# Two of four weight sums of a pair on GpSimd, with signs turned, and other orders in the pairs and ahead of them

## What is computed

```python
h = rms_norm(x, ffn_norm[layer])
gate, up = jnp.split(h @ w_gate_up[layer], 2, axis=-1)
x = x + (jax.nn.silu(gate) * up) @ w_down[layer]
```

## Time and profile before

| | |
|---|---|
| median of 3 runs | 2815.51 us (2812.23 to 2816.04) |
| the profiled execution | 2812.47 us |
| its span (first to last instruction) | 2810.6 us |
| mean granted TensorE clock | 0.988 |
| busy: PE, DVE, ACT, POOL | 2669.9, 1705.8, 1335.0, 1444.9 us |
| three instructions of a pair's four-sum set on raw weights and `w_sum` (L2131, L2134, L2136) | 114.2, 135.9, 115.9 us |

### The profile page before, as it was taken

How to read it: one execution, slowest core, us unless ns; L and a number is a source line. 1 busy time by engine, 2 the same in 40 slices (tenths; PEclk the granted TensorE clock), 3 DMA queues, 4 the chain that set the end, 5 groups by cost and what they waited for, 6 DMA issues and landing times.

```text
span 2810.6 us, 47222 instructions
## 1 busy us (share of the span) xinstructions
PE 2669.9 (95%) x16306; PEld 2328.5 (83%) x16306; DVE 1705.8 (61%) x2881; ACT 1335.0 (47%) x2426; POOL 1444.9 (51%) x953
## 2 busy tenths in 40 slices
PE   9999899999999899999999998999999999899997
PEld 7877889898878889888878887898987888788886
DVE  6674949477454948465545238584757643776674
ACT  7664535356564535353254335353547443453443
POOL 3654456564454556565446434565654473365653
PEclk9999999999999999999999999999999999999998
DMA  4301222333202222232213321322322341132322
GB/s 177 113 2 53 71 95 91 104 113 108 98 24 71 75 95 101 89 128 86 100 43 129 104 66 48 105 90 97 114 96 91 105 150 46 53 109 77 115 75 90
DMA packets 69276, 252.78 MB, mean 90 GB/s; under 512 B 7680, under 2 KB 7936, under 8 KB 68864
## 3 DMA queue, kind: packets, MB, share of 16 engines
q1 hardware_dynamic: 68112, 247.43, 25.6%
q10 hardware_dynamic: 1008, 3.28, 0.4%
HBM read 248.58 MB, written 2.10 MB: 89 GB/s over the span
## 4 chain that ended last, share of the span: by engine, by line
PE 72%; DVE 14%; issue 8%; ACT 4%; DVEq 0%; DMA 0%; POOL 0%; ACTq 0%; SPq 0%; POOLq 0%
PE ps L747 14%; PE ps L749 14%; PE ps L748 14%; PE ps L1140 6%; PE ps L1144 6%; PE ps L1142 6%; PE ps L914 3%; DVE w_sum L2131 2%; PE ps L952 2%; PE ps L937 2%; DVE ps L2139 1%; ACT ev L1557 1%; PE ps L856 1%; DVE w_sum L2134 1%; PE ps L858 1%
## 5 line engine op out<-in xcount | busy, mean ns | idle before, releaser
L628 POOL TENSOR_TENSOR w_lo<-w_raw,w_hi 128x1024 fp32r<-128x1024 f32 x300 | 725.5, 2423 | 710.9 <-ACT w_hi L1377 682.6
L1377 ACT ACTIVATE w_hi<-w_raw 128x1024 fp32r<-128x1024 f32 x302 | 316.9, 1055 | 313.0 <-PE ps L749 237.7
L674 POOL TENSOR_TENSOR w_lo<-w_raw,w_hi 128x512 fp32r<-128x512 f32 x240 | 348.1, 1465 | 169.4 <-ACT w_hi L1361 169.4
L747 PE MATMUL ps<-xh,w_hi 128*128 128x512 f32 x980 | 389.0, 397 | 11.5 <-POOL w_lo L628 4.8
L1140 PE MATMUL ps<-t_hi,w_hi 128*128 128x256 f32 x1280 | 367.3, 287 | 22.3 <-issue 22.3
L749 PE MATMUL ps<-xh,w_lo 128*128 128x512 f32 x980 | 383.3, 391 | 0.0
L748 PE MATMUL ps<-xl,w_hi 128*128 128x512 f32 x980 | 383.1, 391 | 0.0
L1142 PE MATMUL ps<-t_lo,w_hi 128*128 128x256 f32 x1280 | 366.5, 286 | 0.0
L1144 PE MATMUL ps<-t_hi,w_lo 128*128 128x256 f32 x1280 | 366.1, 286 | 0.0
L674 POOL TENSOR_TENSOR w_lo<-w_sum,w_hi 128x512 fp32r<-128x512 f32 x160 | 208.0, 1319 | 299.9 <-ACT w_hi L1361 299.9
L1140 PE MATMUL ps<-xh,w_hi 128*128 128x256 f32 x960 | 278.6, 290 | 59.8 <-ACT ev L1557 55.0
(11 more groups left out here) (342 smaller groups left out, 5708.3 us busy)
## 6 DMA issues: line engine op xcount, KB each, us to landing
w_raw<-weights_in SPq DMA_DIRECT2D x462, 512.0 KB, 3.3
x<-x_in SPq DMA_DIRECT2D x4, 512.0 KB, 7.9
...
rope<-rope_in SPq DMA_DIRECT2D x1, 512.0 KB, 10.9
...
```

The costliest lines, as they stand in the source:

```text
L628: nc.gpsimd.tensor_tensor(w_lo[:, slot], w_raw[:, slot], w_hi.bitcast(f32)[:, slot], ALU.subtract).then_inc(lo_ready, 1)
L674: last = nc.gpsimd.tensor_tensor(quad(w_lo, name, q), src, quad(w_hi, name, q).bitcast(f32), ALU.subtract)
L747: nc.tensor.matmul(dst, w_hi[:, slot, w], hi, start=first, stop=False)
L1377: A(w_hi[:, s], w_raw[:, s], ACT.Copy).then_inc(hi_ready, 1)
```

## The change

- **The sums.** `quad_lows` on POOL begins each pair with sums 3 and 4 (`sums`, semaphore `raw_sums`); DVE keeps sums 2 and 5 (semaphore `bank_sums`). Sum 3 is now +(a + b) instead of -(a + b), so that a plain TENSOR_TENSOR does; sum 2 comes out as before, sum 5 with its sign turned. Products 3 and 5 so have the other sign, and DVE's additions of `ev[2]` and of bank c become subtractions. The sums of a part's first pair stand on POOL right ahead of its low parts, behind the low parts of the chunks before.
- **ACT in a pair.** `ev[2]` is copied right after `ev[1]`; then come `ahead(2)`, `ahead(3)` and `ahead(4)`, and only then the high part of the hidden tile. `ahead(3)` and `ahead(4)` wait for POOL's sums alone.
- **DVE in a pair.** No raw sums ahead; the hidden product behind the addition that follows product 4, and the hidden low part behind those that follow product 5.
- **Ahead of the first pair.** ACT makes the high parts of products 2 to 5 ahead of the first silu. DVE makes sums 2 and 5 right behind `combined_low(1)` (blocks 0 and 1) or behind the first two evictions (2 and 3), and evicts tile 3 last. In blocks 2 and 3 `combine(2)` and `combined_low(1)` stand ahead of the norm on DVE, and `combined_high(2)` ahead of the root on ACT.

No matmul and no DMA is added, removed or moved on PE or SP.

```diff
@@ -358,7 +358,8 @@
-        quad_lo, quad_lo_sum, sums_ready = sem("quad_lo"), sem("quad_lo_sum"), sem("sums_ready")
+        quad_lo, quad_lo_sum = sem("quad_lo"), sem("quad_lo_sum")
+        raw_sums, bank_sums = sem("raw_sums"), sem("bank_sums")
@@ -665,7 +666,21 @@
 
             def quad_lows(name):
 
+                def sums(pair, i):
+
+                    g, c = PAIR0[name] + pair, CHUNK0[name] + 2 * pair
+                    for a in (c, c + 1):
+                        pool.wait_ge(w_in[a % RING], chunk_at(16 * (a // RING + 1), i, 16) - (0 if i is None else 16))
+                    if g:
+                        pool.wait_ge(bank_sums, pair_at(2 * g, i, 2))
+                        pool.wait_ge(quad_lo, pair_at(4 * g, i, 4))
+                    nc.gpsimd.tensor_tensor(SUM_OF[3], raw(name, pair, 1, 0), raw(name, pair, 1, 1),
+                                            ALU.add).then_inc(raw_sums, 1)
+                    nc.gpsimd.tensor_tensor(SUM_OF[4], raw(name, pair, 0, 0), raw(name, pair, 1, 0),
+                                            ALU.subtract).then_inc(raw_sums, 1)
+
                 def body(pair, i):
+                    sums(pair, i)
                     for q in range(QUADS):
                         if q in (2, 5):
                             continue
@@ -1353,8 +1368,10 @@
                 if q in (0, 6):
                     raw_in(c + (q == 6), i)
                 if q in SUM_OF:
-                    n = 4 * g + {3: 1, 4: 2, 2: 4, 5: 4}[q]
-                    act.wait_ge(sums_ready, pair_at(n, i, 4))
+                    if q in (3, 4):
+                        act.wait_ge(raw_sums, pair_at(2 * g + q - 2, i, 2))
+                    else:
+                        act.wait_ge(bank_sums, pair_at(2 * g + 2, i, 2))
                 src = SUM_OF[q] if q in SUM_OF else raw(name, pair, q == 6, q != 0)
                 free = product_done(name, pair - 1, q) if pair else quad_free(name, q)
                 act.wait_ge(chunk_done, pair_at(free, i, QUADS))
@@ -1520,20 +1537,18 @@
                 combined_high(1)
                 gain_part(3, gname)
                 if name in TOGETHER:
+                    combined_high(2)
                     root_rows()
                     high(c0 + LEAD + 1)
                 else:
                     root()
                     high(c0 + LEAD + 1)
-                combined_high(2)
+                    combined_high(2)
+                high(c0 + LEAD + 2)
                 combined_high(3)
-                for j in range(CLASSIC):
-                    if j:
-                        high(c0 + 2 * j + LEAD)
-                        high(c0 + 2 * j + 1 + LEAD)
-                    if j < CLASSIC - 1:
-                        classic_silu(f, j)
-                        classic_high(j)
+                high(c0 + LEAD + 3)
+                classic_silu(f, 0)
+                classic_high(0)
 
             def classic_silu(f, j):
                 act.wait_ge(evac_done, BANK0[f"gu{f}"] + 2 * j + 2)
@@ -1585,14 +1600,14 @@
                         classic_silu(f, CLASSIC - 1)
                     ahead(1)
                     copy_part(pair, i, 1, 2, "a")
-                    ahead(2)
                     copy_part(pair, i, 2, 3, "c")
-                    ahead(3)
+                    for q in (2, 3, 4):
+                        ahead(q)
                     if pair:
                         hidden_high(pair - 1, i)
                     elif part == "a":
                         classic_high(CLASSIC - 1)
-                    for q in range(4, QUADS):
+                    for q in (5, 6):
                         ahead(q)
                     if last:
                         silu(pair, i)
@@ -2117,31 +2132,20 @@
 
             def sum_weights(name, pair, which, i=None):
 
-                g, c = PAIR0[name] + pair, CHUNK0[name] + 2 * pair
-                n = 4 * g
-                if which == 3:
-                    for a in (c, c + 1):
-                        dve.wait_ge(w_in[a % RING], chunk_at(16 * (a // RING + 1), i, 16) - (0 if i is None else 16))
-                if g and which in (3, 4):
-                    dve.wait_ge(quad_lo, pair_at(4 * (g - 1) + which, i, 4))
-                if which in (2, 5):
-                    dve.wait_ge(sums_ready, pair_at(n + (1 if which == 2 else 3), i, 4))
-                dst = SUM_OF[which]
-                if which == 3:
-                    ins = V.scalar_tensor_tensor(out=dst, in0=raw(name, pair, 1, 0), scalar=-1.0,
-                                                 in1=raw(name, pair, 1, 1), op0=ALU.mult, op1=ALU.subtract)
-                elif which == 4:
-                    ins = V.tensor_tensor(dst, raw(name, pair, 0, 0), raw(name, pair, 1, 0), ALU.subtract)
-                elif which == 2:
-                    ins = V.scalar_tensor_tensor(out=dst, in0=SUM_OF[3], scalar=-1.0,
-                                                 in1=raw(name, pair, 0, 0), op0=ALU.mult, op1=ALU.subtract)
+                g = PAIR0[name] + pair
+                if g:
+                    dve.wait_ge(quad_lo_sum, pair_at(2 * (g - 1) + (1 if which == 2 else 2), i, 2))
+                if which == 2:
+                    dve.wait_ge(raw_sums, pair_at(2 * g + 1, i, 2))
+                    ins = V.tensor_tensor(SUM_OF[2], SUM_OF[3], raw(name, pair, 0, 0), ALU.subtract)
                 else:
-                    ins = V.tensor_tensor(dst, raw(name, pair, 0, 1), SUM_OF[2], ALU.subtract)
-                ins.then_inc(sums_ready, 1)
-
-            def sums_of_first(name, which=(3, 4, 2, 5)):
-                for q in which:
-                    sum_weights(name, 0, q)
+                    dve.wait_ge(bank_sums, pair_at(2 * g + 1, i, 2))
+                    ins = V.tensor_tensor(SUM_OF[5], SUM_OF[2], raw(name, pair, 0, 1), ALU.subtract)
+                ins.then_inc(bank_sums, 1)
+
+            def sums_of_first(name):
+                sum_weights(name, 0, 2)
+                sum_weights(name, 0, 5)
 
             def low_of_sum(name, pair, q, i=None):
                 dve.wait_ge(hi_ready, pair_at(product_done(name, pair, q), i, QUADS))
@@ -2162,23 +2166,28 @@
                 combined_low(0)
                 if f < 2:
                     inverse_rms(rstd, 1e-5)
+                    combine(2, gname)
+                    combined_low(1)
                 else:
+                    combine(2, gname)
+                    combined_low(1)
                     inverse_rms_kept(1e-6)
-                combine(2, gname)
-                combined_low(1)
-                sums_of_first(first, (3, 4))
-                evict(0)
-                evict(1)
+                    evict(0)
+                    evict(1)
+                sums_of_first(first)
+                if f < 2:
+                    evict(0)
                 combine(3, gname)
+                if f < 2:
+                    evict(1)
+                low_of_sum(first, 0, 2)
                 combined_low(2)
-                sums_of_first(first, (2, 5))
                 combined_low(3)
+                evict(2)
+                low_of_sum(first, 0, 5)
                 classic_product(0)
-                low_of_sum(first, 0, 2)
                 classic_low(0)
-                evict(2)
                 evict(3)
-                low_of_sum(first, 0, 5)
 
             def classic_product(j):
                 dve.wait_ge(silu_ready, n_.silu.next())
@@ -2229,8 +2238,6 @@
                     def added(what):
                         dve.wait_ge(ev_added, pair_at(6 * g + ADDED[what] + EV_FIRST, i, 6))
 
-                    ahead(3)
-                    ahead(4)
                     done(1)
                     copied(0)
                     V.tensor_tensor(b, b, ev[:, 0], ALU.add).then_inc(ev_added, 1)
@@ -2238,25 +2245,25 @@
                     added("b")
                     V.tensor_tensor(up[:, first], b, rstd[:, first], ALU.mult).then_inc(ev_added, 1)
                     ahead(5)
+                    done(4)
+                    copied(2)
+                    V.tensor_tensor(gate[:, second], a, ev[:, 2], ALU.subtract).then_inc(ev_added, 1)
                     if pair:
                         hidden_product(pair - 1, i)
                     elif part == "a":
                         classic_product(CLASSIC - 1)
-                    done(4)
-                    copied(2)
-                    V.tensor_tensor(gate[:, second], a, ev[:, 2], ALU.add).then_inc(ev_added, 1)
                     low_ahead(2)
+                    done(5)
+                    copied(1)
+                    V.tensor_tensor(c, ev[:, 1], c, ALU.subtract).then_inc(ev_added, 1)
+                    added("a")
+                    V.tensor_tensor(gate[:, second], gate[:, second], rstd[:, second], ALU.mult)
+                    added("c")
+                    V.tensor_tensor(up[:, second], c, rstd[:, second], ALU.mult).then_inc(ev_added, 1)
                     if pair:
                         hidden_low(pair - 1, i)
```

(7 more changed lines are left out.)

## The result

The changed kernel takes **2747.43 us** (median of 4 runs, 2744.94 to 2749.32) against 2814.73 us of the kernel before (2812.23 to 2816.04) beside it: ratio 0.9761, 95% interval 0.9744 to 0.9778. The forecast of 2739 us was 8.4 us too low, and its own range of 2732 to 2746 was missed by 1.4 us; the wider range, 2731 to 2762, holds it. The profiled execution has a time of 2748.38 us, 64.1 us less than the one shown of before; its span is 2746.1 us, 64.5 us less. One of the 21 runs of the kernel before beside the experiments further down took 6108.6 us and is left out of the comparisons.

The account below looks back on a forecast made before the run. The prediction took the kernel as bound by matmuls on PE, with its standstills to win: 65.3 + 1.6 + 6.8 = 73.7 us off 2812.47 gives 2739 us; own range 2732 to 2746, wider range 2731 to 2762.

Parts of the forecast that it names:

- Steady pairs: Pairs after a block's first: each drops from 11.10 us to PE's pace of 10.08, 64 x 1.02 = 65.3 us won.
- Either alone would open the ring: In a pair, moving DVE's sums to POOL or copying `ev[2]` ahead of `ahead(2)` would each suffice to end the 1.02 us loss.
- the ring: In a pair, DVE's sums delay ACT's `ahead(2)` and copy `ev[2]`, then PE's product 5, then DVE's next round: 1.02 us lost.
- POOL at 9.3 us of 10.08: In a pair, POOL's seven instructions at 1.27 us plus 0.44 for one collision with DVE take 9.3 us, within PE's 10.08.
- Rivals 1 and 2: POOL bounds the pairs: first, mildly, 2779 us, chance 0.08; second, held up by the port, slower at 2874 us, chance 0.03.
- Rival 3: In the pairs, DVE's sum 2 waits for POOL's sums, so low parts stay late: about 2805 or 2765 us, chance 0.07.
- First pairs of blocks 0 and 1: PE goes on 0.7 us later before the third product but loses its wait before product 5: net 0.8 us won, twice.
- three `t_lo` at 1.2 ... and eight `t_f` steps at 0.45: DVE's list behind `rstd` in first pairs of blocks 0 and 1: 3.6 + 3.6 us of the 12.0 us counted.
- The wait ahead of product 5: PE's wait in the first pairs of blocks 0 and 1, up to 1.7 us, was to go as everywhere.
- First pairs of blocks 2 and 3: PE goes on 1.8 us sooner despite a late norm, plus 1.6 us at product 5: 3.4 us won, twice.
- The "issue" waits: Four PE waits, one in each block's first pair, forecast at 4.5 to 5 us each.
- Rival 4: First pairs: PE's new stop at the norm and the 0.50 clock lose 2 us a block: 2755 us, chance 0.12.

Follow-up runs that it names:

- `e_low_wait`: The changed kernel, with POOL's low part of product 3 in each block's first pair waiting for DVE's last `t_lo` tile: 2738.97 us, ratio 0.9734.

## Why the prediction was right or wrong, point by point

- **Steady pairs, 65.3 us: right in the period, 3 pairs too many in the count, and lucky in the product.** The period went from 11.10 to 10.08 us, and the stretches from one block's second pair to the next norm saved 63.3 us. I had multiplied 1.02 by 64 pairs. But in the trace of before three pairs of block 2, two in part a and one in part b, take 10.08 us already: that block saved 12.5 us, where the others saved 16.2 to 17.7. The earlier trace rows had said so: 65 waits for `ev`, less one in each of four first pairs, are 61. 61 x 1.02 = 62.2 would have been the term. By the starts of the pairs these 61 saved 64.7 us, 1.06 each, since the first two pairs of parts b and c took 11.22 and 11.15 us and not 11.10: the count was too high and the price too low, and the two nearly cancelled. The 1.4 us between 64.7 and 63.3 were lost behind the pairs, where nothing was changed; this differs from run to run (in block 2 the stretch saves 11.5 to 13.7 us in the runs whose pairs take 10.08).
- **"Either alone would open the ring, I think; both together surely": half right.** The copy's place alone does it, 10.08 us. The sums on POOL alone leave 10.20. I had left the ring's sum unmade for each part alone: product 1 to the copy is 3.98 us without the long sums, and with 5.76 us of PE and what lies between them that is 10.20, over 10.08. The sentence hid that the costlier part of the change isn't needed in a steady pair.
- **POOL at 9.3 us of 10.08, idle 0.7 or more: right.** 9.2 us, idle 0.79. Rivals 1 and 2 didn't come, but the run with an eighth instruction shows how near rival 1 was. Sum 2 on DVE at 1.77 us lies in the 1.4 to 1.8 named.
- **Rival 3, the port rule: out in the pairs, true in the first ones.** What decides is whether anything waits for the DVE step that is held up.
- **First pairs of blocks 0 and 1, 0.8 us won each: wrong, 1.0 and 0.9 us lost.** The step that failed is "three `t_lo` at 1.2 ... and eight `t_f` steps at 0.45". I had counted the collision of POOL's sums (2.2 us; the norm's `rstd` is ready 1.95 us later, right), but not that ACT's new order releases POOL's low parts of products 3 and 4 into these very steps. They cost 2.09 us, and `e_low_wait` gives 2.0 of them back. The copy comes 2.6 us later instead of 0.7. The wait ahead of product 5 did go: product 2 to 5 takes 6.76 us after 8.30, the 1.5 us that the net of 0.8 us implies.
- **First pairs of blocks 2 and 3, 3.4 us won each: the mechanism right, the size half.** The broadcast waits 2.5 us (I said 2.6), the wait ahead of the pair is gone. Product 2 begins 0.5 us sooner where I had 1.8: again a `t_f` step held up, 1.1 us by `e_low_wait`. At product 5 1.3 us went, not 1.6. The "issue" waits, for which I had named 4.5 to 5 us each, are 5.5 us in blocks 0 and 1 and 6.3 in 2 and 3.
- **The sum.** Of the 9.6 us between 73.7 and 64.1, the first pairs are 8.4 - 1.8 = 6.6, the stretches with the steady pairs 65.3 - 63.3 = 2.0, and what lies ahead of the first norm and around the span 0.6 + 0.4 = 1.0. The range that holds the result is the wide one, which was stretched for rivals 3 and 4; that it held rests on the size of the loss and not on their mechanisms. Rival 4 had the place of the loss in blocks 0 and 1, with another mechanism: not PE's stop at the norm, but DVE's list. "PE's idle time in front of the first pairs' third product grows" was my own sign of being wrong, and it did in blocks 0 and 1, 5.07 us to 5.47, beside the new 1.7 us ahead of product 1.
